# Three column sums of squares taken by one product each: more adds on GpSimd, and two of the sums placed later

## The reference

```
h = rms_norm(x, norm_mix_g)            # opening norm of a layer
x = x + hybrid_mixer(h)                # conv module, dilated attention of 4 heads, short conv, gates, w_o
h = rms_norm(x, norm_x_g)
mem_n = rms_norm(mem, norm_mem_g)      # 256 memory tokens
x = x + memory_cross_attention(h, mem_n)
h = rms_norm(x, norm_ffn_g)            # feed-forward norm
x = x + swiglu(h)                      # layer one
x = x + moe_swiglu(h)                  # layer two: top 2 of 8 experts
return rms_norm(x, final_g)
```

## Time and profile before

| | us |
|---|---|
| median of 3 runs | 1905.89 (1905.44 to 1907.44) |
| the profiled execution | 1905.4 |
| its span | 1903.6 |
| TensorE busy | 1890.4 |
| VectorE busy | 1540.5 |
| ScalarE busy | 1225.4 |
| GpSimd busy | 70.6 |

### The profile page before, as it was taken

The page is one execution under the profiler, slowest core; times in us unless marked ns, Lnnn a source line. Parts: engine busy times, 40 slices in busy tenths (PEclk is TensorE's granted clock), DMA queues, the critical chain, the costliest instruction groups (busy, mean ns, idle before and its releaser), DMA issues.

```text
span 1903.6 us, 27279 instructions
## 1 busy us (share of the span) xinstructions
PE 1890.4 (99%) x10806; PEld 1655.3 (87%) x10806; DVE 1540.5 (81%) x1395; ACT 1225.4 (64%) x1095; POOL 70.6 (4%) x80
## 2 busy tenths in 40 slices
PE   9999999999999999999999999999999999999998
PEld 9989999999999988999988888888888888888886
DVE  8999865565568999764688888888888888888886
ACT  6555745454455565654577777777777777777775
POOL 1000000100010000000000000000000000000000
PEclk9999999999999999999999999999999999999999
DMA  9544544355545435553699999999999999999993
GB/s 338 182 159 145 188 162 181 133 189 183 192 165 187 166 133 197 179 184 127 244 363 384 378 384 363 406 373 379 374 359 401 378 374 385 352 412 373 375 397 113
DMA packets 76265, 521.39 MB, mean 274 GB/s; under 512 B 9360, under 2 KB 9616, under 8 KB 14992
## 3 DMA queue, kind: packets, MB, share of 16 engines
q1 hardware_dynamic: 72464, 507.84, 69.9%
q0 software_dynamic: 2992, 11.01, 2.0%
q10 hardware_dynamic: 720, 1.31, 0.2%
HBM read 512.79 MB, written 7.34 MB: 273 GB/s over the span
## 4 chain that ended last, share of the span: by engine, by line
PE 89%; DVE 5%; ACT 3%; issue 1%; DMA 0%; SPq 0%; ACTq 0%; DVEq 0%
PE psum L1671 21%; PE psum L1673 21%; PE psum L1672 21%; PE psum L1685 14%; PE psum L1686 7%; DVE wlo L1036 2%; ACT whi L564 2%; PE psum L2137 1%; PE psum L1893 1%; PE psum L1913 1%; PE psum L1832 1%; DVE U L1144 1%; DMA raw<-in_stream 0%; DVE U L1059 0%; PE psum L1810 0%
## 5 line engine op out<-in xcount | busy, mean ns | idle before, releaser
L1036 DVE TENSOR_TENSOR wlo<-raw,whi 128x2048 fp32r<-128x2048 f32 x477 | 1086.4, 2283 | 253.7 <-ACT whi L564 253.4
L564 ACT ACTIVATE whi<-raw 128x2048 fp32r<-128x2048 f32 x477 | 909.5, 1909 | 245.7 <-PE psum L1673 195.3
L1671 PE MATMUL psum<-whi,act_hl 128*128 128x512 f32 (+1 forms) x1472 | 567.5, 386 | 0.8
L1673 PE MATMUL psum<-whi,act_hl 128*128 128x512 f32 (+1 forms) x1472 | 560.2, 381 | 0.0
L1672 PE MATMUL psum<-wlo,act_hl 128*128 128x512 f32 (+1 forms) x1472 | 559.5, 380 | 0.0
L1685 PE MATMUL psum<-h_hl,whi 128*128 128x512 f32 x1216 | 431.5, 399 | 0.3 <-DVE U L1385 0.2
L1686 PE MATMUL psum<-h_hl,wlo 128*128 128x256 f32 x1216 | 340.4, 280 | 0.0
L1671 PEld LDWEIGHTS psum<-whi,act_hl 128*128 128x128 f32 x1472 | 276.9, 188 | 55.6 <-DVE wlo L1036 4.1
L1673 PEld LDWEIGHTS psum<-whi,act_hl 128*128 128x128 f32 x1472 | 276.8, 188 | 53.6
L1672 PEld LDWEIGHTS psum<-wlo,act_hl 128*128 128x128 f32 x1472 | 277.1, 188 | 51.4 <-issue 0.7
L1685 PEld LDWEIGHTS psum<-h_hl,whi 128*128 128x128 f32 x1216 | 228.4, 188 | 55.4 <-issue 0.7
(11 more groups left out here) (252 smaller groups left out, 1393.6 us busy)
## 6 DMA issues: line engine op xcount, KB each, us to landing
raw<-in_stream SPq DMA_DIRECT2D x474, 1024.0 KB, 6.7
raw<-in_stream SPq DMA_DIRECT2D x6, 512.0 KB, 3.7
U<-in_stream SPq DMA_DIRECT2D x2, 1024.0 KB, 11.8
xacc<-U POOLq DMA_DIRECT2D x3, 512.0 KB, 5.9
xT<-in_x_cols ACTq DMA_DIRECT2D x4, 256.0 KB, 6.7
raw<-in_stream SPq DMA_DIRECT2D x4, 256.0 KB, 7.5
memhat<-in_mem_cols SPq DMA_DIRECT2D x1, 1024.0 KB, 18.5
hrow<-U POOLq DMA_DIRECT2D x1, 1024.0 KB, 5.3
```

The costliest lines, as they stand in the source:

```text
L564: act.activation(whi[:, n % SPLIT, 0:words], src[:, 0:words], ACT.Copy).then_inc(hi_ready, 1)
L1036: dve.tensor_tensor(wlo[:, n % SPLIT, 0:words], src[:, 0:words], whi[:, n % SPLIT, 0:words].bitcast(F32), ALU.subtract).then_inc(lo_ready, 1)
L1671: pe.matmul(o, st[0], mv[0], start=start, stop=False, **kw)
L1673: return pe.matmul(o, st[1], mv[0], start=False, stop=stop, **kw)
```

## The change

For q = 2 and q = 3 (`WHOLE`) GpSimd also adds the fourth pair, seven adds in all, and TensorE takes one product of the one block that is left. The memory's four sums are added into one as well, seven adds instead of four, and one product. The sum of the feed-forward norm is placed behind the first chunk's last product, that of layer two's opening norm halfway through chunk 2, and that of the memory ahead of chunk 9; its root, its reciprocal and its scaling come two chunks later too.

```diff
+WHOLE = (2, 3)
+
+def added(q):
+    return sum(7 if m in WHOLE else 5 for m in SUMMED if m < q)
@@ gpsimd, sums(q)
-                before = 5 * SUMMED.index(q)
-                for pair in range(3):
+                before = added(q)
+                for pair in range(4 if q in WHOLE else 3):
@@ gpsimd, the memory
                         gp.tensor_tensor(msq[:, 2 * k, :], msq[:, 2 * k, :], msq[:, 2 * k + 1, :], ALU.add).then_inc(msq_sum, 1)
+                        if k:
+                            gp.wait_ge(msq_sum, 2 * k)
+                            gp.tensor_tensor(msq[:, 0, :], msq[:, 0, :], msq[:, 2 * k, :], ALU.add).then_inc(msq_sum, 1)
@@ scalar, after_split(n): the memory's root
-                if n == 6:
+                if n == 8:
@@ vector, post(n): its reciprocal, the scaling of memhat
-                if n == 6:
+                if n == 8:
...
-                if n in (7, 8):
+                if n in (9, 10):
                     settled()
-                    some = memhat[:, 4 * n - 28:4 * n - 24, :]
+                    some = memhat[:, 4 * n - 36:4 * n - 32, :]
@@ tensor, norm_pair(q, pair)
+                if q in WHOLE:
+                    if pair == 3:
+                        pe.wait_ge(sq_sum, added(q) + 7)
+                        pe.matmul(norm_bank(q)[:, 0:256], ones[:], sq[:, 0, :], start=True, stop=True).then_inc(ss_done, 1)
+                    return
                 if q in SUMMED and pair < 3:
                     if pair == 2:
-                        pe.wait_ge(sq_sum, 5 * SUMMED.index(q) + 5)
+                        pe.wait_ge(sq_sum, added(q) + 5)
@@ tensor, the loop over the plan
-                    if c == 2:
-                        norm(3 * lay)
-                    if n == 7:
-                        pe.wait_ge(msq_sum, 4)
-                        stat(msq[:, 0:DB:2, :], DB // 2).then_inc(mss_done, 1)
+                    if c == 2 and lay == 0:
+                        norm(0)
+                    if n == 9:
+                        pe.wait_ge(msq_sum, 7)
+                        stat(msq, 1).then_inc(mss_done, 1)
...
                     elif unscaled(n):
-                        chunk_in(n, of=xg_parts)
+                        chunk_in(n, midway=(lambda: norm(3)) if lay and c == 2 else None, of=xg_parts)
@@ tensor, the feed-forward
-                    opening_in(f, 2, bank[4], lambda: norm(2))
+                    opening_in(f, 2, bank[4])
+                    norm(2)
```

## The result

| | changed kernel | kernel before, in the same comparison |
|---|---|---|
| first comparison, median (range) | 1913.52 us (1911.88 to 1914.34, 7 runs) | 1906.03 (1905.33 to 1908.36, 7 runs) |
| second comparison (run e11) | 1911.96 (1911.55 to 1913.24, 9 runs) | 1907.26 (1904.67 to 1909.41, 20 runs) |
| ratio, 95% interval | 1.0036 [1.0024, 1.0047]; second 1.0025 [1.0015, 1.0035] | |
| the profiled execution | 1912.84, span 1911.1 | 1905.4, span 1903.6 |

The forecast was +3.6 us, 1909.5. The change costs 7.5 us in the first comparison and 4.7 in the second; 1913.52 lies above the range given, and the time is slower by more than 0.2%.

The account below looks back on a forecast made before the run. TensorE, busy 99% of the span, was taken as the bound, with waits on VectorE/ScalarE chains. Memory +1.6, feed-forward norm 0 and layer two's norm +2.0 gave +3.6 us: 1909.5, 0.19% slower; range 1905.5 to 1912.5.

Parts of the forecast that it names:

- the one that kept the clock out of the sum: Argument that TensorE's pause before chunk 7 brings no clock fall, as page slices around two existing pauses show none.
- the stretch: Before chunk 7: three more GpSimd adds slow VectorE's small operations and delay its subtraction, +1.2 us (bounds 0 and 2.2).
- The rival's price: Clock falls after TensorE's 3.5 us pause before chunk 7: 3.4 us or half, total 1911.2 to 1912.9; chance 0.18.
- The memory's product: Ahead of chunk 9: the one product that comes back stands where TensorE does not wait, +0.43 us.
- The removed products: Ahead of chunk 7: taking the memory's four products away only lengthens TensorE's wait for the low part, worth 0.
- Root, reciprocal and scaling two chunks later: Memory's chain up to the first head's attention: later root fits with 1.7 us of slack remaining, cost 0.
- rival (d): Layer one's first head: attention stalls because the 1.7 us slack is missing, up to 2 us more, 1911; chance 0.07.
- Feed-forward norm: TensorE's 0.86 us gain only lengthens its wait at 394.07, worth 0 (bounds -0.9 to +0.3).
- Layer two's norm: Opening norm: root 2.03 us later, a chain without slack to the eighth chunk, +2.0 us (bounds -0.9 and +2.9).
- (a): Whole kernel: TensorE's time counts and other work fills the waits, -3.0 us, 1902.9; chance 0.08.
- (b): Memory and layer two's norm: only one of the two chains costs, 1906.5 to 1908; chance 0.12.
- The adds don't hold it: Layer two's opening norm: the last two adds end at about 573.7, before the product at 574.11.

Follow-up runs that it names:

- e11: The changed kernel once more, unaltered, against the kernel before: 1911.96 us against 1907.26, ratio 1.0025.
- e1: Kernel before with only the memory's edits (seven adds, one product ahead of chunk 9, root and scaling two chunks later): 1910.29 us against 1906.53, ratio 1.0024.
- e4: Changed kernel with 18 idle products of 128 columns ahead of chunk 7: 1910.64 us against 1906.53 for the kernel before, ratio 1.0021.
- e5: Kernel before with the memory's sum, root and scaling two chunks later, still four adds and four products: 1909.49 us against 1906.4, ratio 1.0013.
- e9: Kernel before with the memory's seven adds after chunk 8's split, one product ahead of chunk 10, root and scalings later: 1906.15 us against 1907.26, ratio 0.9993.
- e2: Kernel before with only layer two's opening norm changed (seven adds, one product, half a chunk later): 1908.57 us against 1906.53, ratio 1.0007.
- e7: Kernel before with layer two's norm only moved half a chunk later, still five adds and three products: 1909.72 us against 1906.4, ratio 1.0013.
- e8: Kernel before with layer two's norm at seven adds and one product, ahead of chunk 2 as before: 1907.86 us against 1906.4, ratio 1.0009.
- e6: Kernel before with seven adds and one product for the memory, ahead of chunk 7 as before: 1909.78 us against 1906.4, ratio 1.0017.

## Why the prediction was wrong

**The step that failed is the one that kept the clock out of the sum: "Against: no slice around the pauses before 53.15 and 394.07 shows a fall".** The memory's sum ended with the stretch. The stretch itself was right (1.39; three adds at 0.48 each), and the pause was foreseen (3.5 us forecast, 3.71 measured). What the pause does to the clock was left out of the sum and put among the rivals with 0.18. It measured 2.5 us in the first profile of the change, 1.5 in the second and 1.6 in e1, and e4 takes it away. In the timed runs the clock takes 4.8 us more than before in the first comparison and 2.0 in the second. Without it 2.7 us are left in both (7.5 - 4.8 and 4.7 - 2.0), or up to 3.6 in the first, where 0.9 us of the fall lie in the pause; the forecast's sum was 3.6. So the terms that it did price were not far off, and the one it left out carried the time past the range. The rival's price was of the right size (the windows show 1.7 and 3.4 us of fall, of which 1.5 and 2.5 hit products), its chance was not.

The step rested on two pauses that were read off the page's slices. They last 0.6 and 0.47 us, so they said nothing on one of 3.7; and a slice of 48 us hides a fall, since the loss of (1 - 0.51) x 7 = 3.4 us moves its mean by 0.07. In the changed kernel too the row of clocks on the page shows 9 in all places. The fall was visible only in windows of a few microseconds. The Trainium skill ("TensorE: Matmul & The Clock Gate", Part 1) says that an idle engine falls to the slow clock and that activity lifts it; the trace agrees, 0.51 after 3.71 us without a product and 1.00 in e4 with idle ones. The one fall that the prediction set beside that rule is weaker support than it says: the earlier trace rows has TensorE busy for 5.00 of 5.00 us there, with narrow products.

Point by point:
- The memory's product, +0.43: right. The removed products, 0: right in the change, but e5 shows what stood behind that zero: they filled a gap, and without them TensorE idles 2.21 us and the clock falls.
- The stretch, +1.2: 1.39. By the Trainium skill ("SBUF — State Buffer", Who interferes with whom) a whole instruction would be lost to each add, an estimate of 3 x 0.74 = 2.2 us; the trace shows 3.59 - 2.15 = 1.44 for three adds, 0.48 each, two thirds of that. The first four adds cost about as much: e9 against the earlier trace rows gives 3.85 - 2.40 = 1.45, and some three of the four (46.48 to 49.43) fall beside VectorE's small operations, which begin at 47.12.
- Root, reciprocal and scaling two chunks later, 0: right; the slack of 1.7 us sufficed (1.8 measured), no stall in the first head, rival (d) did not occur.
- Feed-forward norm, 0: +0.3 or less. TensorE's 0.86 went into the wait for the low part, which grew from 0.47 to 1.33, just as much. The 0.3 is no more than two profiles of one kernel differ by.
- Layer two's norm, +2.0: +1.8, root +2.01. The chain without slack is confirmed from two sides (e2 and e7: root 1.7 and 2.7 later, TensorE 1.8 and 2.8 late at the experts); e8 is held by TensorE's own wait and a fall of the clock. "The adds don't hold it" is true only because the product stands so late: in its old place it waits for them (e8), and the root is no earlier.
- (a), TensorE's time counts, -3.0: refuted in all three places. (b), only one chain costs: e1 and e2 show both.
- What is left: with 4.2 + 1.8 + 0.3 the parts make 6.3 us, the first comparison has 7.5 and the second 4.7. The gap between the two comparisons is the clock's: the runs of the first lose 10.7 us by it and those of the second 8.1, 2.6 of the 2.8 us. (The kernel before in the first comparison has no clocks on record; it is taken at 5.9, as in the others.) Why the clock falls for longer in one comparison than in the other is open.

The sum as it should have stood: 1.4 (stretch) + 0.4 (product) + 2.0 (clock, the middle of 1.5 and 2.5) + 0 + 1.9 = 5.7 us, between the two comparisons' 4.7 and 7.5.

## What to carry to other kernels

A product that TensorE takes while it waits anyway costs nothing, and may be worth more than nothing: it keeps the engine from an idle stretch after which it runs at half its clock for a while (3.3 to 5.6 us here, from the first product behind the pause). Before taking work out of a gap, or lengthening one, look at the granted clock in windows of a few microseconds, not in the page's slices, and price the fall as part of the sum. Adds handed to GpSimd are paid by VectorE, about 0.5 us each where VectorE is in a row of small operations on which TensorE waits; put them where VectorE is in nothing urgent (e9), not where their inputs come ready.

## What the runs showed of the hardware that was not expected

- Pauses of TensorE of 1.23 (e9), 1.33 and 1.46 us (changed kernel and e2) left the clock at 1.00; those of 2.21 (e5), 2.27 (e8) and 3.7 us (changed kernel, e1, e11) were each followed by a fall. (The 2.29 us before TensorE's first product, at the very start of the span, were not.)
- The first part of the pause is still at full clock in the records (1.00 from 50 to 53); the lower level comes late in it and stays while TensorE is at work again, until 60.0 in the changed kernel and, after the 2.21 us of e5, until 56.7. One product of 0.25 us in the middle of a pause (e6: 1.26 us idle, the product, 1.79 us idle) did not prevent it.
- TensorE at work can fall too. In the changed kernel, 32 products with 10 columns each stand ahead of the later fall, one every 0.11 us, in which the engine counts as busy. That they bring the fall is not shown: the same 32 products stand in the three profiles without it.

```profile
956.49 3.64 PE L2090 MATMUL psum<-U 128*128 128x10 f32 x32
...
960.98 0.47 PE L1684 MATMUL psum<-wlo,act_hl 128*128 128x512 f32 x1
961.25 0.63 PE L1685 MATMUL psum<-whi,act_hl 128*128 128x512 f32 x1
```

- The same program, the kernel before, showed losses of 3.4 and of 1.8 us by such falls in two executions, and its spans without them were equal within 0.2 us.
